# A two-model transformer kernel: its weight ring as one tensor of eight places, and as eight buffers at eight different offsets

## The chip, the cores and the metric

The kernel runs on one core of one Trainium2 chip. The metric is the device time of one launch in microseconds, as the median of three runs. A "slot" below is a piece of the weight stream, not a time.

## What is computed

Two blocks follow each other on a sequence of 256 rows of width 1024, all in float32. The first block has one S5 state-space layer and one attention layer; the second block has two layers with three branches each (latent attention, convolution, retention) and a gated feed-forward part. Cut to what matters here:

```python
def first_block(x, norm_g, ...):
    for i in range(DEPTH):                    # 2
        hn = rms_norm(h, norm_g[i])
        y = s5_mixer(hn, ...) if i % 2 == 0 else moba_mixer(hn, ...)
        h = h + y

def second_block(x, ...):
    for l in range(DEPTH):                    # 2
        h = rms_norm_2(x, ln_mix_pre[l])
        proj = h @ w_in[l]
        ...
        merged = gates[:, :, 0] * y_mla + gates[:, :, 1] * y_conv + gates[:, :, 2] * y_ret
        x = x + rms_norm_2(merged @ w_out[l], ln_mix_post[l])
        h = rms_norm_2(x, ln_ffn_pre[l])
        f = (jax.nn.silu(h @ ffn_w_gate[l]) * (h @ ffn_w_up[l])) @ ffn_w_down[l]
        x = x + rms_norm_2(f, ln_ffn_post[l])
```

Nearly all of the work is the product of 256 rows with some 200 MB of weights, each of which is used once.

## The kernel before

`weight_plan` (the table at the top of the file) cuts all weight matrices into slots in the order in which they are used. A slot is two k-tiles of 128 rows by up to 512 columns: 128 partitions by 1024 numbers, 4 KB in each partition, 512 KB in all. The narrow ones are the slots of the latent projection (two k-tiles by 416 columns) and of the query projection `uq` (384 columns).

Each slot goes through four steps, on four engines, and each engine does its step slot after slot:

- SyncE issues the load of the slot into its place of the ring (L1225, `weights_raw`), once the slot that had the place before is used.
- ScalarE writes the high part, rounded to the TensorE's fast 32-bit type float32r (L1244, `weights_hi<-weights_raw`).
- VectorE writes the rest, the number minus its high part, also in float32r, over the raw numbers (L1776, `weights_lo<-weights_raw,weights_hi`).
- TensorE multiplies. A product is the sum of three: high by high, low by high, high by low.

The activations are kept transposed, also as a high and a low part: `act_F_hi/lo` for most projections, `ffn_F_hi/lo` (hidden part of the feed-forward), `mla_F_hi/lo` and `conv_F_hi/lo`. There are two forms of the product:

- `tile_slot` (L700, L701, L702): the activation tile of 128 by 128 is the stationary operand, the weights are the moving one, 512 columns (416 or 384 in the narrow slots). The profile prints the two in the order moving, stationary: `acc<-weights_hi,act_F_hi`.
- `hidden_slot` (L678, L679, L680): the weights are the stationary operand, 128 by 128, and the activations the moving one, 256 columns. This is the form of the feed-forward's first products, two attention projections and the convolution's input: `acc<-act_F_hi,weights_hi`.

The first 16 slots (`whole_slot`, L639) are multiplied in plain float32 from `weights_raw` against `hn_F`, with no high and low part.

While a matmul streams its moving operand, TensorE already loads the stationary operand of the next one. In `tile_slot` each matmul has another stationary tile than the one before, and so it is in `hidden_slot`.

The ring has six places, `R = 6`, and two more, `R_MORE = 2`, in three stretches of the program in which there is room for them (`weights_hi_more` and so on, the attention, and each layer from its latent heads' end on). `place` gives each slot the place that was filled longest ago. A ring is one tensor `[P, R, SLOT]`; a place is 4096 bytes, so all its places begin at the same offset modulo 512 bytes. `weights_raw` and `weights_lo` lie at the same addresses. Small tensors that nothing reads (`weights_offset` L205, `rows_offset` L261, `latent_rows_offset`, `conv_rows_offset` and `mla_heads`) push what follows them to another offset. The three functions `high`, `whole` and `low` (L233 to L243) give the operand of a slot from its place. Nothing else names the ring.

Of the kernel before, what the change touches and what calls it, by code (L numbers as in the profile page):

```python
# [8 lines left out]
F32 = mybir.dt.float32  # L9
F32R = mybir.dt.float32r  # L10
# [5 lines left out]
P = 128  # L16
# [34 lines left out]
R, R0 = 6, 4  # L51

R_MORE = 2
AHEAD = R - 2
SLOT = 1024

WHOLE = 16

# [11 lines left out]
def weight_plan():  # L70


    chunks = []

    def add(name, n, width, ktiles):
        slots = [(k, min(2, ktiles - k)) for k in range(0, ktiles, 2)]
        for i in range(n):
            chunks.append((f"{name}{i}", width, slots))

    add("ssm_in.", 4, 512, DT)  # L80
    add("glu.", 2, 512, DT)
    add("ssm_out.", 2, 512, DT)
    for i in ATTN_ORDER:
        chunks.append((f"attn_in.{i}", 512, [(k, 2) for k in range(0, DT, 2)]))
    add("attn_out.", 2, 512, DT)
    for l in range(DEPTH2):
        add(f"L{l}.lat.", 1, QR + KVR + ROPE, DT)
        add(f"L{l}.glu.", 2, 512, DT)
        add(f"L{l}.uq.", 2, 384, QR // P)
        add(f"L{l}.ukv.", 2, 512, KVR // P)  # L90
        add(f"L{l}.ret.", 6, 512, DT)
        add(f"L{l}.gate.", 6, 512, DT)
        add(f"L{l}.mla_o.", 2, 512, 4)
        add(f"L{l}.ret_o.", 2, 512, DT)
        add(f"L{l}.conv_o.", 2, 512, 4)
        add(f"L{l}.out.", 2, 512, DT)
        add(f"L{l}.ffn.", HID // FCH, 2 * FCH, DT)
        add(f"L{l}.down.", 2, 512, HT)
    slot, off, table, slots = 0, 0, {}, []
    for c, (name, width, parts) in enumerate(chunks):  # L100
        table[name] = dict(index=c, width=width, first=slot, n=len(parts))
        for k, nk in parts:
            slots.append(dict(chunk=name, k=k, nk=nk, width=width, off=off))
            off += P * nk * width
            slot += 1
    return table, slots, off
# [68 lines left out]
def build(nc, stream, consts, x_in, ssm_ab, ssm_ldt, ssm_bc, rows, qk_gain, positions, decay, conv_p, lat_gain, out):  # L175
    table, slots, _ = weight_plan()
# [16 lines left out]
    with ctx:  # L193
        def sb(name, shape, dt=F32, scope=None):
            return (scope or ctx).enter_context(nc.sbuf_tensor(name, shape, dt))
# [6 lines left out]
        with_channels = [name for name in table if ".ffn." in name or name in ("attn_in.6", "attn_in.7")  # L202
                         or (name[0] == "L" and ".glu." in name)]

        sb("weights_offset", [P, 16])  # L205
        with ExitStack() as s0:
            sb("weights_near", [P, R0, SLOT], F32, s0)
            bcq = sb("ssm_by_pair", [P, 4, Q, GROUP], F32, s0)
        with ExitStack() as s0:
            raw = sb("weights_raw", [P, R, SLOT], F32, s0)  # L210
        w_lo = sb("weights_lo", [P, R, SLOT], F32R)
        with ExitStack() as s0:
            c_alt = sb("c_mats_alt", [P, 4, PQ, SUB * GROUP], F32, s0)
            f0 = sb("hn_F", [P, DT, SEQ], F32, s0)
        w_hi = sb("weights_hi", [P, R, SLOT], F32R)

        begins = [table["attn_in.0"]["start"]] + [table[f"L{l}.lat.0"]["start"] + MLA_END for l in range(DEPTH2)]
        ends = [table[f"L{l}.uq.0"]["start"] for l in range(DEPTH2)] + [NS]
        place, last_in = [], {}
# [8 lines left out]
        for a in begins:  # L228
            for p in range(R, R + R_MORE):
                n = min(n for n in range(a + R, NS) if place[n] == p)  # L230
                before[n] = max(a, before[n] or 0)

        def high(n, cols):  # L233

            return w_hi[:, place[n], cols] if place[n] < R else hi_more[:, place[n] - R, cols]

        def whole(n, cols):

            return raw[:, place[n], cols] if place[n] < R else raw_more[:, place[n] - R, cols]

        def low(n, cols):

            return w_lo[:, place[n], cols] if place[n] < R else lo_more[:, place[n] - R, cols]  # L243
        const = sb("consts", [P, N_CONST])
        ident = const[:, C_ID:C_ID + P]
        xT = sb("x_T", [P, TT, D])
# [11 lines left out]

        sb("rows_offset", [P, 16])  # L261
        with ExitStack() as s0:
            toep = sb("toeplitz", [P, 2, SUB, PCOLS], F32, s0)
        f_hi = sb("act_F_hi", [P, DT, SEQ], F32R)
# [57 lines left out]
        with ExitStack() as s4:  # L322
            latp = sb("lat_gain", [P, QR + KVR], F32, s4)
            cfp = sb("conv_params", [P, 4, TAPS + 3], F32, s4)
            sb("latent_rows_offset", [P, 24], F32, s4)
            mo_hi = sb("mla_F_hi", [P, 4, SEQ], F32R, s4)
            mo_lo = sb("mla_F_lo", [P, 4, SEQ], F32R, s4)
            c_hi, c_lo = mo_hi, mo_lo
            conv_t = sb("conv_tanh", [P, TT, CONV], F32, s4)
            conv_F = sb("conv_in_F", [P, 4, SEQ + 2 * PAD], F32, s4)  # L330
            conv_sum = sb("conv_acc_F", [P, 4, SEQ], F32, s4)
            bns = sb("bn_stats", [P, 10, 8], F32, s4)
            rope_w = conv_t[:, 0, :].rearrange("p (k h d) -> p k h d", k=4, h=MLA_H)
            rqT = sb("ret_q_T", [P, TT, 512], F32, s4)
            rkT = sb("ret_k_T", [P, TT, 512], F32, s4)
            ret_g = sb("ret_g_T", [P, TT, D], F32, s4)
            gates = sb("gates_T", [P, 3, TT, D], F32, s4)

            with ExitStack() as s5:
                cT = sb("lat_T", [P, TT, QR + KVR + ROPE], F32, s5)  # L340
                cnT = sb("lat_norm_T", [P, TT, QR + KVR], F32, s5)
            r_d = sb("r_decay_T", [P, RH, TT, SEQ], F32, s4)
            with ExitStack() as s5:
                mq = sb("mla_q_T", [P, TT, MLA_H, MQK], F32, s5)
                mk = sb("mla_k_T", [P, TT, MLA_H, MQK], F32, s5)
                mv = sb("mla_v_T", [P, TT, MLA_H, MV], F32, s5)
                m_qk = sb("m_qk_F", [P, 2, 512], F32, s5)
                m_p = sb("m_probs", [P, 2, TT, SEQ], F32, s5)
                m_pt = sb("m_probs_T", [P, 2, TT, TT, P], F32, s5)
                m_st = sb("m_stat", [P, 2, 8], F32, s5)  # L350

            with ExitStack() as s6:
                r_qk = sb("r_qk_F", [P, RH, 512], F32, s6)
                r_s = sb("r_scores_T", [P, 2, TT, SEQ], F32, s6)
            with ExitStack() as s6:
                sb("conv_rows_offset", [P, 24], F32, s6)
                cf_hi = sb("conv_F_hi", [P, 4, SEQ], F32R, s6)
                cf_lo = sb("conv_F_lo", [P, 4, SEQ], F32R, s6)
            with ExitStack() as s6:
                sb("mla_heads", [P, 3880], F32, s6)  # L360
                hi_more = sb("weights_hi_more", [P, R_MORE, SLOT], F32R, s6)
                with ExitStack() as s7:
                    raw_more = sb("weights_raw_more", [P, R_MORE, SLOT], F32, s7)
                lo_more = sb("weights_lo_more", [P, R_MORE, SLOT], F32R, s6)
        rv = hT
        gF = hT[:, :, :].rearrange("p t d -> p (t d)").rearrange("p (h q) -> p h q", q=SEQ)

# [866 lines left out]
        def _(act):  # L1234
            pos = 0

            def make_hi(s):
                n = slots[s]["nk"] * slots[s]["width"]
                if s < WHOLE:
                    return  # L1240
                act.wait_ge(raw_in[place[s]], landed(s))
                if s < WHOLE + R:
                    act.wait_ge(slot_used, WHOLE)
                act.activation(high(s, slice(0, n)), whole(s, slice(0, n)), ACT.Copy).then_inc(hi_made, 1)  # L1244
# [1595 lines left out]
```

## Time and profile before

| | us |
|---|---|
| median of 3 runs | 1238.23 |
| lowest, highest | 1234.74, 1239.33 |
| span of the profiled execution | 1235.8 |
| TensorE busy in it | 1205.2 |
| VectorE busy | 901.5 |
| ScalarE busy | 639.1 |
| GpSimd busy | 100.4 |

No time of the profiled execution beyond its span is given; the span lies between the lowest run and the median. Times in the profile are counted from the span's start. The duration that is shown for a matmul (0.39 us for 512 columns) contains its latency, and the next matmul starts before it ends. So what a matmul costs in a stream is the distance from its start to the start of the next, called its pitch here. A row of the timeline is one instruction or several alike in a row; its first number is its start. The distance of two far starts by the number of matmuls between them gives a pitch to a tenth of a nanosecond.

### The profile page before, as it was taken

To read this page: it belongs to the slowest core of one execution; us is meant where nothing else is said; L and a number is where in the kernel's file an instruction comes from. 1 tells how busy PE (TensorE), PEld (TensorE's weight loads), DVE (VectorE), ACT (ScalarE), POOL (GpSimd) and SP (SyncE) were. 2 spreads that over 40 slices of the span, in tenths; PEclk is the share of its full clock that TensorE was granted. 3 is DMA by queue.
4 is the path that set the end of the run, shared out by engine and by line. 5 is a ranking of instruction groups with operands and counts; after the bars stand their busy time and mean duration, and the time that the engine had idled before them with its cause. 6 is when DMAs were issued, how large, how long until landed. Compare 5 with 4: busy or idle time off the path is not lost.

```text
span 1235.8 us, 19035 instructions
## 1 busy us (share of the span) xinstructions
PE 1205.2 (98%) x7597; PEld 1013.5 (82%) x7597; DVE 901.5 (73%) x1463; ACT 639.1 (52%) x1034; POOL 100.4 (8%) x163
## 2 busy tenths in 40 slices
PE   7999999999999999999999999999999999999998
PEld 3566778888988788787999987988788787999986
DVE  7998877757589998687666655589997687665553
ACT  4334565665556665545444544556575545444441
POOL 6300011101000200201000001000200201000000
PEclk9999999999999999999999999999999999999999
DMA  7635666434565555354766664565445355565552
GB/s 251 221 94 173 205 208 191 156 119 146 163 205 168 155 157 187 133 169 164 216 201 188 193 195 154 174 211 169 158 153 188 132 170 170 190 197 193 191 194 75
DMA packets 71958, 215.68 MB, mean 175 GB/s; under 512 B 16256, under 2 KB 19744, under 8 KB 71744
## 3 DMA queue, kind: packets, MB, share of 16 engines
q1 hardware_dynamic: 65008, 206.37, 52.0%
q0 software_dynamic: 2112, 6.97, 1.8%
q10 hardware_dynamic: 4752, 1.14, 0.4%
q8 instruction: 60, 0.98, 0.3%
q14 instruction: 26, 0.21, 0.1%
HBM read 208.95 MB, written 3.15 MB: 172 GB/s over the span
## 4 chain that ended last, share of the span: by engine, by line
PE 86%; DVE 8%; ACT 3%; issue 2%; POOL 1%; DMA 0%; DVEq 0%; POOLq 0%; ACTq 0%
PE acc L700 17%; PE acc L702 17%; PE acc L701 17%; PE acc L678 7%; PE acc L680 7%; PE acc L679 7%; PE acc L639 3%; PE mixed L1015 1%; DVE weights_lo L1776 1%; PE mixed L1112 1%; ACT junk L1279 1%; PE turned L755 1%; DVE h_T L1806 1%; PE mixed L999 1%; PE mixed L1008 1%
## 5 line engine op out<-in xcount | busy, mean ns | idle before, releaser
L1776 DVE TENSOR_TENSOR weights_lo<-weights_raw,weights_hi 128x1024 fp32r<-128x1024 f32 (+1 forms) x304 | 355.7, 1204 | 71.6 <-ACT weights_hi L1244 71.0
L1244 ACT ACTIVATE weights_hi<-weights_raw 128x1024 fp32r<-128x1024 f32 (+1 forms) x304 | 305.8, 1043 | 80.8 <-DMA weights_raw<-stream_dram 80.6
L700 PE MATMUL acc<-weights_hi,act_F_hi 128*128 128x512 f32 (+1 forms) x680 | 275.7, 406 | 5.6 <-DVE act_F_lo L1806 3.4
L702 PE MATMUL acc<-weights_hi,act_F_lo 128*128 128x512 f32 (+1 forms) x680 | 267.2, 393 | 0.0
L701 PE MATMUL acc<-weights_lo,act_F_hi 128*128 128x512 f32 (+1 forms) x680 | 265.4, 390 | 0.0
L678 PE MATMUL acc<-act_F_hi,weights_hi 128*128 128x256 f32 x624 | 173.6, 278 | 0.0
L679 PE MATMUL acc<-act_F_hi,weights_lo 128*128 128x256 f32 x624 | 172.5, 276 | 0.0
L680 PE MATMUL acc<-act_F_lo,weights_hi 128*128 128x256 f32 x624 | 172.4, 276 | 0.0
L700 PEld LDWEIGHTS acc<-weights_hi,act_F_hi 128*128 128x128 f32 x680 | 128.7, 189 | 34.2 <-DVE act_F_lo L1806 4.3
L702 PEld LDWEIGHTS acc<-weights_hi,act_F_lo 128*128 128x128 f32 x680 | 128.4, 189 | 28.4
L701 PEld LDWEIGHTS acc<-weights_lo,act_F_hi 128*128 128x128 f32 x680 | 128.7, 189 | 25.6
L679 PEld LDWEIGHTS acc<-act_F_hi,weights_lo 128*128 128x128 f32 x624 | 117.2, 188 | 0.2
L678 PEld LDWEIGHTS acc<-act_F_hi,weights_hi 128*128 128x128 f32 x624 | 117.1, 188 | 0.2
L680 PEld LDWEIGHTS acc<-act_F_lo,weights_hi 128*128 128x128 f32 x624 | 117.2, 188 | 0.0
L1806 DVE SCALAR_TENSOR_TENSOR conv_acc_F<-conv_in_F,conv_params,conv_acc_F 128x256 f32<-128x256 f32 x240 | 97.9, 477 | 0.0
L1776 DVE TENSOR_TENSOR weights_lo_more<-weights_raw_more,weights_hi_more 128x1024 fp32r<-128x1024 f32 (+1 forms) x60 | 71.4, 1214 | 18.2 <-ACT weights_hi_more L1244 18.1
L1806 DVE SCALAR_TENSOR_TENSOR ffn_tanh_F<-ffn_tanh_F,acc 128x512 f32<-128x512 f32 (+1 forms) x24 | 15.4, 643 | 89.4 <-ACT ffn_tanh_F L1364 84.8
L1244 ACT ACTIVATE weights_hi_more<-weights_raw_more 128x1024 fp32r<-128x1024 f32 (+1 forms) x60 | 61.9, 1048 | 26.8 <-DMA weights_raw_more<-stream_dram 26.8
L1364 ACT ACTIVATE ffn_tanh_F<-acc 128x512 f32<-128x512 f32 x20 | 12.0, 598 | 111.3 <-PE acc L680 111.3
L639 PE MATMUL acc<-weights_raw,hn_F 128*128 128x512 f32 x128 | 59.9, 615 | 1.0 <-ACT hn_F L1380 1.0
L678 PE MATMUL acc<-act_F_hi,weights_hi_more 128*128 128x256 f32 x208 | 57.7, 277 | 0.0
L680 PE MATMUL acc<-act_F_lo,weights_hi_more 128*128 128x256 f32 x208 | 57.4, 276 | 0.0
(339 smaller groups left out, 1923.6 us busy)
## 6 DMA issues: line engine op xcount, KB each, us to landing
weights_raw<-stream_dram SPq DMA_DIRECT2D x306, 512.0 KB, 3.7
weights_raw_more<-stream_dram SPq DMA_DIRECT2D x58, 512.0 KB, 4.3
gains<-rows_dram POOLq DMA_DIRECT2D x12, 512.0 KB, 4.8
weights_raw<-stream_dram SPq DMA_DIRECT2D x6, 416.0 KB, 3.1
weights_raw<-stream_dram SPq DMA_DIRECT2D x4, 384.0 KB, 3.5
x_T<-x_in_dram SPq DMA_DIRECT2D x4, 256.0 KB, 6.0
ssm_bc<-ssm_bc_dram SPq DMA_DIRECT2D x1, 1024.0 KB, 8.6
u_scratch<-u_T ACTq DMA_DIRECT2D x4, 256.0 KB, 5.5
```

What stands on the lines that cost most here:

```text
L639: i = pe.matmul(acc[par][t][:, 0:w], f0[:, k, t * P:(t + 1) * P], whole(pos, slice(kk * w, (kk + 1) * w)), start=first and kk == 0, stop=l ...
L678: pe.matmul(o, wh, hi[:, k, :], start=first and kk == 0 and m % 2 == 0, stop=False, skip_group_check=True)
L679: pe.matmul(o, wl, hi[:, k, :], start=False, stop=False, skip_group_check=True)
L680: i = pe.matmul(o, wh, lo[:, k, :], start=False, stop=last and kk == s["nk"] - 1, skip_group_check=True)
L700: pe.matmul(o, xh, wh, start=first and kk == 0, stop=False)
L701: pe.matmul(o, xh, wl, start=False, stop=False)
L702: i = pe.matmul(o, xl, wh, start=False, stop=last and kk == s["nk"] - 1)
L755: i = pe.transpose(turned_bank[n % 2][:, kk * P:(kk + 1) * P], src(t, 4 * half + kk), ident)
L999: x = pe.transpose(b[0:dk, (2 * n + t) * P:(2 * n + t + 1) * P], src(t, i), ident)
L1244: act.activation(high(s, slice(0, n)), whole(s, slice(0, n)), ACT.Copy).then_inc(hi_made, 1)
L1776: dve.tensor_tensor(low(s, slice(0, n)), whole(s, slice(0, n)), high(s, slice(0, n)).bitcast(F32), ALU.subtract).then_inc(lo_made, 1)
L1806: return dve.scalar_tensor_tensor(out=o, in0=a, scalar=s, in1=b, op0=op0, op1=op1)
```

## The change

The tensors of the ring become lists of tensors, one for each place: a to f for the six, g and h for the two more. Each but the last of a list is 16 numbers (64 bytes) longer than a slot, so that the next place begins 64 bytes further modulo 512. The padding tensor before the ring goes; one of 8 numbers now stands between the low and the high part; `rows_offset` goes; the two places g and h get paddings so that they continue the rows of offsets. No instruction is added, removed or moved: on all five engines the same instructions stand in the same order with the same waits, and the loads have the same sizes. Only addresses differ.

```diff
+LINE = 16
...
-        sb("weights_offset", [P, 16])
+        def places(names, kind, dt, scope=None):
+
+            return [sb(f"weights_{kind}_{c}", [P, SLOT + LINE], dt, scope) for c in names[:-1]] + [
+                sb(f"weights_{kind}_{names[-1]}", [P, SLOT], dt, scope)]
+
         with ExitStack() as s0:
-            sb("weights_near", [P, R0, SLOT], F32, s0)
+            sb("weights_near", [P, R0, SLOT + LINE], F32, s0)
             bcq = sb("ssm_by_pair", [P, 4, Q, GROUP], F32, s0)
         with ExitStack() as s0:
-            raw = sb("weights_raw", [P, R, SLOT], F32, s0)
-        w_lo = sb("weights_lo", [P, R, SLOT], F32R)
+            raw = places("abcdef", "raw", F32, s0)
+        w_lo = places("abcdef", "lo", F32R)
+        sb("weights_offset", [P, 8])
...
-        w_hi = sb("weights_hi", [P, R, SLOT], F32R)
+        w_hi = places("abcdef", "hi", F32R)
...
-            return w_hi[:, place[n], cols] if place[n] < R else hi_more[:, place[n] - R, cols]
+            return w_hi[place[n]][:, cols] if place[n] < R else hi_more[place[n] - R][:, cols]
...
-        sb("rows_offset", [P, 16])
...
-                sb("mla_heads", [P, 3880], F32, s6)
-                hi_more = sb("weights_hi_more", [P, R_MORE, SLOT], F32R, s6)
+                sb("mla_heads", [P, 3912], F32, s6)
+                hi_more = places("gh", "hi", F32R, s6)
+                sb("low_offset", [P, 24], F32, s6)
                 with ExitStack() as s7:
-                    raw_more = sb("weights_raw_more", [P, R_MORE, SLOT], F32, s7)
-                lo_more = sb("weights_lo_more", [P, R_MORE, SLOT], F32R, s6)
+                    raw_more = places("gh", "raw", F32, s7)
+                lo_more = places("gh", "lo", F32R, s6)
```

`whole` and `low` change as `high` does. Where the tensors begin, in bytes modulo 512:

| | before | after |
|---|---|---|
| raw and low part, places a to h | 192 in all | 128, 192, 256, 320, 384, 448, 0, 64 |
| high part, places a to h | 192 in all | 480, 32, 96, 160, 224, 288, 352, 416 |
| `act_F_hi/lo`, `ffn_F_hi/lo`, `conv_F_hi/lo` | 128 | 160 |
| `mla_F_hi/lo` | 256 | 288 |
| `hn_F` | 192 | 480 |

A k-tile of 512 columns, a tile of 128 columns and a k-tile of activations are whole multiples of 512 bytes, so within a slot these offsets hold for every operand. The second k-tile of a slot of 416 columns begins 1664 bytes in, which is 128 modulo 512.

## Rows read from the trace of the kernel before

**Rows 1.** The page: the span, TensorE's share, and its granted clock in 40 slices.

```profile
span 1235.8 us, 19035 instructions
...
PE 1205.2 (98%) x7597; PEld 1013.5 (82%) x7597; DVE 901.5 (73%) x1463; ACT 639.1 (52%) x1034; POOL 100.4 (8%) x163
...
PEclk9999999999999999999999999999999999999999
```

**Rows 2.** The page: the chain that ended last, by engine.

```profile
PE 86%; DVE 8%; ACT 3%; issue 2%; POOL 1%; DMA 0%; DVEq 0%; POOLq 0%; ACTq 0%
```

**Rows 3.** TensorE's groups by line and shape: count | busy us, mean ns | idle before.

```profile
L700 PE MATMUL acc<-weights_hi,act_F_hi 128*128 128x512 f32 x656 | 267.0, 407 | 5.4 <-DVE act_F_lo L1806 3.4 <-DVE weights_lo L1776 2.0
...
L678 PE MATMUL acc<-act_F_hi,weights_hi 128*128 128x256 f32 x624 | 173.6, 278 | 0.0
...
L678 PE MATMUL acc<-act_F_hi,weights_hi_more 128*128 128x256 f32 x208 | 57.7, 277 | 0.0
...
L700 PE MATMUL acc<-weights_hi,ffn_F_hi 128*128 128x512 f32 x144 | 55.9, 388 | 0.0
...
L700 PE MATMUL acc<-weights_hi,mla_F_hi 128*128 128x512 f32 x24 | 9.6, 402 | 0.0
```

**Rows 4.** TensorE's waits: for which instruction, us in total, times, longest.

```profile
PE acc L700 <- DVE weights_lo L1776: 2.2, 5, 0.7
```

**Rows 5.** Timeline, feed-forward's second product of layer 0: first and last matmul.

```profile
702.99 0.39 PE L700 MATMUL acc<-weights_hi,ffn_F_hi 128*128 128x512 f32 x1
...
763.18 0.40 PE L702 MATMUL acc<-weights_hi,ffn_F_lo 128*128 128x512 f32 x1
```

**Rows 6.** Timeline, product with `mla_F` in layer 0: second and last matmul of a stretch.

```profile
507.34 0.39 PE L701 MATMUL acc<-weights_lo,mla_F_hi 128*128 128x512 f32 x1
...
512.47 0.39 PE L702 MATMUL acc<-weights_hi,mla_F_lo 128*128 128x512 f32 x1
```

**Rows 7.** Timeline, a slot of 416 columns: second k-tile from 307.50, first of the next from 308.06.

```profile
307.50 0.35 PE L700 MATMUL acc<-weights_hi,act_F_hi 128*128 128x416 f32 x1
...
308.06 0.35 PE L700 MATMUL acc<-weights_hi,act_F_hi 128*128 128x416 f32 x1
...
308.63 0.35 PE L700 MATMUL acc<-weights_hi,act_F_hi 128*128 128x416 f32 x1
```

**Rows 8.** Timeline, `hidden_slot` in layer 0's feed-forward: first and last matmul of a stretch.

```profile
605.17 0.28 PE L679 MATMUL acc<-act_F_hi,weights_lo 128*128 128x256 f32 x1
...
702.87 0.28 PE L680 MATMUL acc<-act_F_lo,weights_hi_more 128*128 128x256 f32 x1
```

**Rows 9.** Busy us (and instructions) of each engine in stretches, then clock, DMA share, GB/s.

```profile
core 0: us, PE busy (x) PEld busy (x) DVE busy (x) ACT busy (x) POOL busy (x), PEclk, DMA share, GB/s
702.99:763.18 60.19, 60.19 (x265) 49.40 (x264) 31.60 (x31) 26.83 (x35) 1.57 (x4) 1.00 0.57 173
605.17:702.87 97.70, 97.70 (x864) 97.70 (x863) 58.66 (x63) 44.15 (x54) 0.00 (x0) 1.00 0.64 194
507.34:512.47 5.13, 5.13 (x23) 4.11 (x22) 2.77 (x6) 3.64 (x9) 2.95 (x6) 1.00 0.24 68
...
754.97:758.11 3.14, 3.14 (x15) 2.60 (x14) 0.00 (x0) 0.00 (x0) 0.00 (x0) 1.00 0.03 10
736.99:740.48 3.49, 3.49 (x17) 2.87 (x16) 3.49 (x4) 2.27 (x3) 0.00 (x0) 1.00 0.73 181
```

**Rows 10.** Timeline, a stretch with the other engines idle, and one with them busy.

```profile
737.09 0.39 PE L702 MATMUL acc<-weights_hi,ffn_F_lo 128*128 128x512 f32 x1
...
740.29 0.39 PE L701 MATMUL acc<-weights_lo,ffn_F_hi 128*128 128x512 f32 x1
...
755.17 0.39 PE L700 MATMUL acc<-weights_hi,ffn_F_hi 128*128 128x512 f32 x1
...
757.92 0.39 PE L700 MATMUL acc<-weights_hi,ffn_F_hi 128*128 128x512 f32 x1
```

**Rows 11.** The page: the two steps that make the parts of a slot, and its load.

```profile
L1776 DVE TENSOR_TENSOR weights_lo<-weights_raw,weights_hi 128x1024 fp32r<-128x1024 f32 (+1 forms) x304 | 355.7, 1204 | 71.6 <-ACT weights_hi L1244 71.0
L1244 ACT ACTIVATE weights_hi<-weights_raw 128x1024 fp32r<-128x1024 f32 (+1 forms) x304 | 305.8, 1043 | 80.8 <-DMA weights_raw<-stream_dram 80.6
...
weights_raw<-stream_dram SPq DMA_DIRECT2D x306, 512.0 KB, 3.7
```

More of the change, by code:

```diff
@@ L233, in high @@
         def high(n, cols):
-            return w_hi[:, place[n], cols] if place[n] < R else hi_more[:, place[n] - R, cols]
+            return w_hi[place[n]][:, cols] if place[n] < R else hi_more[place[n] - R][:, cols]
         def whole(n, cols):
-            return raw[:, place[n], cols] if place[n] < R else raw_more[:, place[n] - R, cols]
+            return raw[place[n]][:, cols] if place[n] < R else raw_more[place[n] - R][:, cols]
         def low(n, cols):
-            return w_lo[:, place[n], cols] if place[n] < R else lo_more[:, place[n] - R, cols]
+            return w_lo[place[n]][:, cols] if place[n] < R else lo_more[place[n] - R][:, cols]
         const = sb("consts", [P, N_CONST])
```

## The prediction

> **What bounds the kernel.** I read the page first: TensorE is busy for 1205.2 of 1235.8 us, at the full clock in all slices [rows 1], and the chain that ended last runs through it for 86% of the span [rows 2]. Its waits come next: for the low part of a slot, the last product of the ring's pipeline, it waits 2.2 us in all [rows 4]. So neither loads, nor ScalarE, nor VectorE set the pace: the time is the number of matmuls by their pitch. The change leaves the instructions as they are, so it can only act through the pitch, or by making the pipeline of the ring so slow that TensorE waits.
>
> For the pitch I went to the timeline. In the feed-forward's second product, 264 matmuls of 512 columns start between 702.99 and 763.18 us: 60.19 us by 263 steps is **228.9 ns** [rows 5]. At the upper of TensorE's two clocks (2.4 GHz, granted in full there [rows 9]) 512 columns are 213.3 ns; 15.6 ns are left over. In the hidden form 97.70 us by 862 steps (864 instructions of the window less two still running at its start) is **113.3 ns** for 256 columns [rows 8, 9], with 6.7 ns left over. What these leftovers hang on is the whole question.
>
> **Do the other engines make them?** The places of the ring now all begin at the same offset, so one could think that TensorE, reading one place, meets ScalarE, VectorE or a load in the same part of another. The trace has a clean test of it. From 754.97 to 758.11 us VectorE, ScalarE and GpSimd are idle and the DMA share is 0.03; 12 steps there take 2.75 us, 229.2 ns each. From 736.99 to 740.48 us VectorE is busy all the time, ScalarE for 2.27 us, the DMA share is 0.73; 14 steps take 3.20 us, 228.6 ns each [rows 9, 10]. The other engines cost a matmul nothing that I can see.
>
> **Do TensorE's own two reads make them?** While a matmul streams its moving operand, the next stationary one is loaded. I call relation the start of the moving operand minus that of the stationary one being loaded, modulo 512 bytes. Before, it is 64 for the tile form (192 minus 128), except 448 with `mla_F` (192 minus 256), 192 in the second k-tile of a 416-column slot, and 448 in the hidden form (128 minus 192). With `mla_F`, 5.13 us by 22 steps is 233.2 ns [rows 6, 9]: 4.3 ns more than at relation 64. In the slots of 416 columns three steps at relation 192 take 0.56 us and the next three, at relation 64, 0.57 us [rows 7]; that is 186.7 against 190.0 ns, 3.3 less at 192, known only to some 3 ns since starts are given to 10 ns. So the relation does matter, by some 2% of a matmul between the best and the worst of three, and this is what the change spreads.
>
> The Trainium skill says otherwise: its page "SBUF — State Buffer", section "Who interferes with whom", gives TensorE two independent read ports, one for the moving operand and one for the weight load, and says that it never waits on anyone. By that the sum would be exactly zero. The two pitches at the same shape speak against it, the quiet stretch for its other half.
>
> **The terms.** After the change the relation of the high part takes, over the places a to h, 320, 384, 448, 0, 64, 128, 192 and 256: all eight. The low part takes eight that lie half-way between them (480, 32, 96, 160, 224, 288, 352, 416). Only 64, 192 and 448 have rows. I take the mean of these three as the mean of all.
>
> - Tile form at 64: 656, 80, 144, 32 and 32 instructions of L700 with 512 columns (the largest and one other in [rows 3]), 944, by the three lines, 2832 matmuls. The three relations give 228.9, 225.6 (3.3 less, from the 416-column rows) and 233.2: mean 229.2. 2832 by 0.3 ns is **+0.9 us**. Bounds: all at the best, 2832 by -3.3, -9.3 us; all at the worst, 2832 by 4.3, +12.2 us. I take the mean since the places are used in turn.
> - Tile form with `mla_F`: 24 and 16 by three, 120 matmuls, from 233.2 to 229.2: **-0.5 us**. Slots of 416 columns: 96 matmuls that had one good and one middling relation and get the mean: 0, within 96 by 4 ns, 0.4 us. Those of 384 columns: 48, likewise within 0.2 us.
> - Hidden form: 624 and 208 instructions of L678 [rows 3], by three 2496 matmuls at 113.3 ns, at relation 448. That is the worst of the three in the tile form, whose leftover is 19.9 ns there and 15.9 in the mean, a factor of 0.8. If the leftover of 6.7 ns shrinks alike, a matmul gains 1.3 ns: **-3.3 us**. Here the roles are exchanged and no row shows another relation. Lower bound: the leftover shrinks as 12.3 to 19.9 at the best relation, 2.6 ns, -6.5 us. Upper bound: nothing excludes that 448 is good in this form, so the same 2.6 ns upwards, +6.5 us. I take the middle of the gain, since the direction of the difference is the same.
> - The first 16 slots in plain float32, transposes and attention: their operands' relations change too, but 128 matmuls and small shapes are all; 0, within 1 us.
> - ScalarE and VectorE: both work inside one place; the high part now begins 352 bytes further modulo 512 than the raw one. L1776 takes 1204 ns and L1244 1043 [rows 11]. Even 3% on both, some 35 ns, on a slot that lasts 12 matmuls (2.7 us) is covered: VectorE is idle for 71.6 us ahead of this very step, and TensorE waits 2.2 us for it. If that cover went, 364 slots by 35 ns would be 13 us; I cost it at 0. The loads have the same size, still begin at multiples of 64 bytes, and 3.7 us to landing are covered by the ring's depth.
>
> Sum: 0.9 - 0.5 - 3.3 = **-2.9 us**, on a span of 1235.8: 1232.9. The median is 2.4 us above this execution's span, so 1235.3 on the scale of the runs.
>
> **Rival 1, slower: the relations without rows are the bad ones.** Two streams that begin in step (relation 0, and 32 and 480 next to it) may collide longest, and 448 is the nearest to them with a row, and the worst. If five of eight relations cost what 448 does, the tile form pays five eighths of 12.2 us, +7.6; if in the hidden form 448 was a good one and it pays 1.3 ns, +3.2 us. Together +10.8: 1249. For it: the trend from 192 to 64 to 448. Against it: the worst seen is only 4.3 ns. It decides once the mean pitch in the stretch of [rows 5] is above 231 ns.
>
> **Rival 2, faster: most relations are as good as 192.** Then the tile form gains 2.5 ns, -7.1 us, and the hidden one the full 2.6 ns, -6.5 us: 1224.6. For it: 192 lies in the wide gap of five values without rows, and is best; against it: one shape of 96 matmuls carries it.
>
> **Rival 3, faster: the leftovers are collisions with the other engines after all**, and spreading the places removes them: 15.6 ns by 2832 and 6.7 by 2496, up to -61 us, 1177. The quiet stretch speaks against it. The page "TensorE: Matmul & The Clock Gate", section "Back-to-back issue gap" of the Trainium skill, gives 2.5 ns over the columns' time as the gap of a lone stream; its sum here would be some 37 us for the tile form, as an estimate, if something could remove the rest. The trace never shows it for this type.
>
> **Rival 4, nothing at all:** the pitch is a matter of the operands' other properties, `mla_F` differing by chance of its place: 1238.2.
>
> **The numbers.** About what a measurement of this kernel can tell from no change is 0.5%, 6.2 us. My forecast, near the middle, 0.34, and rival 4, 0.06, fall within it, though their own spread leaks to both sides; rival 1 has 0.30, rival 2 0.27, rival 3 0.03. With the leaks this makes 0.32 for faster, 0.36 for the same and 0.32 for slower. The cases of both signs hold most of the chance; the forecast's own range is 1230 to 1241. The whole range reaches from beyond rival 2, 1221, to beyond rival 1, 1255: below lies the tile form's lower bound with the hidden one's (-15.8, 1222), above both upper bounds (+18.7, 1257), not quite reached.
>
> **What would show it.** The clock, the number of instructions and the waits should stay as they are. In the timeline of the feed-forward's second product the pitch should no longer be the same from slot to slot but go through a cycle with the places: groups of 12 matmuls near 226, 229 and 233. If all of them stay at 228.9, rival 4 holds. The hidden stretch of 862 steps should fall from 97.70 to about 96.6 us; if it is above 98, the exchange of roles was the mistake. Stretches with `mla_F` should come down on the mean. If TensorE's wait for the low part grows beyond some 5 us, the cost of L1776 and L1244 was mis-sized. A pitch that changes within a slot with what ScalarE or VectorE does would overturn the argument from the quiet stretch.

## The result and the profile after

The changed kernel takes 1251.78 us (median of 4 runs, 1251.5 to 1253.75), the kernel before 1238.78 on the same chip (4 runs, 1234.74 to 1241.58). The ratio is 1.0118, with a 95% interval of 1.01 to 1.0137: **slower by 1.2%**. The forecast was 1235.3, a gain of 2.9 us; what came is a loss of 13.0 us. The time lies inside the stated range, near its upper end, and within 3 us of rival 1.

The page after, the lines that answer to [rows 1] and [rows 2]:

```profile
span 1251.9 us, 19035 instructions
...
PE 1223.8 (98%) x7597; PEld 1025.6 (82%) x7597; DVE 902.2 (72%) x1463; ACT 637.6 (51%) x1034; POOL 100.4 (8%) x163
...
PEclk9999999999999999999999999999999999999999
...
PE 87%; DVE 8%; ACT 3%; issue 1%; POOL 1%; DMA 0%; DVEq 0%; POOLq 0%; ACTq 0%
```

The instructions are as many, the granted clock is 0.994 over the span where it was 0.995, VectorE and ScalarE are as busy as before to 1.5 us. Only TensorE is busy longer, by 18.6 us, on a span that is 16.1 us longer; the difference is idle time of TensorE that is gone. (The spans differ by more than the medians, since the trace before is of one of the faster executions and the trace after is of the slowest of its four, 1253.75 us.) The line numbers of the changed kernel are 8 higher there: L686 to L688 are the hidden form, L708 to L710 the tile form.

The timeline after, the first and last matmul of the two stretches of [rows 8] and [rows 5]:

```profile
609.13 0.28 PE L687 MATMUL acc<-act_F_hi,weights_lo_a 128*128 128x256 f32 x1
...
710.32 0.28 PE L688 MATMUL acc<-act_F_lo,weights_hi_h 128*128 128x256 f32 x1
710.43 0.40 PE L708 MATMUL acc<-weights_hi_c,ffn_F_hi 128*128 128x512 f32 x1
...
771.55 0.40 PE L710 MATMUL acc<-weights_hi_b,ffn_F_lo 128*128 128x512 f32 x1
```

The hidden form's 862 steps take 101.19 us, 117.4 ns each, where they took 97.70, 113.3 ns. The tile form's 263 steps take 61.12 us, 232.4 ns each, against 228.9. By 2496 matmuls the first is 10.2 us; by 2832 the second is 9.9 us at most, if the other stretches of the tile form lost as much. Together they cover the 18.6 us.

The description of the tile form ahead is wrong in one thing. Its matmuls of L708 and L709 (L700 and L701 before) use the same stationary tile, the high part of the activations, and only L710 has another one. The page shows as many weight loads as matmuls all the same, 7597 each [rows 1]. So what holds in both forms is that each matmul has a load of its own, and not that each has another tile.

Busy time of each engine in three stretches after: one in which only TensorE works, the hidden stretch and the tile stretch.

```profile
core 0: us, PE busy (x) PEld busy (x) DVE busy (x) ACT busy (x) POOL busy (x), PEclk, DMA share, GB/s
762.90:766.36 3.46, 3.46 (x16) 2.81 (x15) 0.00 (x0) 0.00 (x0) 0.00 (x0) 1.00 0.06 24
609.13:710.32 101.19, 101.19 (x865) 101.19 (x863) 58.66 (x63) 44.13 (x54) 0.00 (x0) 1.00 0.60 187
710.43:771.55 61.12, 61.12 (x266) 49.47 (x264) 31.60 (x31) 26.82 (x35) 1.67 (x4) 1.00 0.56 169
```

The timeline of the first of them, with the other engines idle:

```profile
763.17 0.39 PE L710 MATMUL acc<-weights_hi_f,ffn_F_lo 128*128 128x512 f32 x1
...
766.18 0.40 PE L708 MATMUL acc<-weights_hi_e,ffn_F_hi 128*128 128x512 f32 x1
```

Thirteen steps take 3.01 us, 231.5 ns each. The same quiet stretch before had 229.2 [rows 10]. So the loss is there also with VectorE, ScalarE and GpSimd idle and a DMA share of 0.06. All of these steps but the first are in places a and b, whose slots take 231.1 and 232.2 ns a matmul over both layers, so the quiet has made them no faster. And TensorE's waits for the low part have not grown: 2.0 us in five waits, against 2.2 in five before [rows 4]. What VectorE and ScalarE need for a slot is the same within 1%, here for place a:

```profile
PE acc L708 <- DVE weights_lo_c L1784: 0.8, 2, 0.6
...
PE acc L708 <- DVE weights_lo_d L1784: 0.6, 1, 0.6
...
PE acc L708 <- DVE weights_lo_b L1784: 0.6, 2, 0.3
...
L1784 DVE TENSOR_TENSOR weights_lo_a<-weights_raw_a,weights_hi_a 128x1024 fp32r<-128x1024 f32 (+2 forms) x51 | 61.5, 1205 | 11.7 <-ACT weights_hi_a L1252 11.7
...
L1252 ACT ACTIVATE weights_hi_a<-weights_raw_a 128x1024 fp32r<-128x1024 f32 (+2 forms) x51 | 53.2, 1043 | 12.7 <-DMA weights_raw_a<-stream_dram 12.7
```

### The profile page after: what moved, and what is told of

Read it like the earlier page. It is cut to its first block, busy times and chain, and to the rows that moved or that the text cites. A ratio compares the mean times of both kernels' runs of the same rounds, so it can differ in the third digit from the quotient of the medians.

```text
span 1251.9 us, 19035 instructions
## 1 busy us (share of the span) xinstructions
PE 1223.8 (98%) x7597; PEld 1025.6 (82%) x7597; DVE 902.2 (72%) x1463; ACT 637.6 (51%) x1034; POOL 100.4 (8%) x163
## 4 chain that ended last, share of the span: by engine, by line
PE 87%; DVE 8%; ACT 3%; issue 1%; POOL 1%; DMA 0%; DVEq 0%; POOLq 0%; ACTq 0%
PE acc L708 17%; PE acc L709 17%; PE acc L710 17%; PE acc L688 8%; PE acc L687 8%; PE acc L686 7%; PE acc L647 3%; PE mixed L1023 1%; PE mixed L1120 1%; ACT junk L1287 1%; PE turned L763 1%; PE mixed L1007 1%; PE mixed L1016 1%; DVE h_T L1814 1%; DVE junk L1817 1%
## 5 line engine op out<-in xcount | busy, mean ns | idle before, releaser
L1784 DVE TENSOR_TENSOR weights_lo_c<-weights_raw_c,weights_hi_c 128x1024 fp32r<-128x1024 f32 (+2 forms) x51 | 61.8, 1211 | 19.9 <-ACT weights_hi_c L1252 19.4
L1784 DVE TENSOR_TENSOR weights_lo_e<-weights_raw_e,weights_hi_e 128x1024 fp32r<-128x1024 f32 (+3 forms) x50 | 59.9, 1198 | 16.6 <-ACT weights_hi_e L1252 16.6
L1784 DVE TENSOR_TENSOR weights_lo_a<-weights_raw_a,weights_hi_a 128x1024 fp32r<-128x1024 f32 (+2 forms) x51 | 61.5, 1205 | 11.7 <-ACT weights_hi_a L1252 11.7
L1784 DVE TENSOR_TENSOR weights_lo_b<-weights_raw_b,weights_hi_b 128x1024 fp32r<-128x1024 f32 (+2 forms) x51 | 61.4, 1205 | 9.5 <-ACT weights_hi_b L1252 9.5
L1784 DVE TENSOR_TENSOR weights_lo_d<-weights_raw_d,weights_hi_d 128x1024 fp32r<-128x1024 f32 (+2 forms) x51 | 61.7, 1209 | 8.7 <-ACT weights_hi_d L1252 8.5
L1784 DVE TENSOR_TENSOR weights_lo_f<-weights_raw_f,weights_hi_f 128x1024 fp32r<-128x1024 f32 (+3 forms) x50 | 59.9, 1198 | 5.5 <-ACT weights_hi_f L1252 5.4
L1252 ACT ACTIVATE weights_hi_b<-weights_raw_b 128x1024 fp32r<-128x1024 f32 (+2 forms) x51 | 53.2, 1043 | 18.2 <-DMA weights_raw_b<-stream_dram 17.9
L1252 ACT ACTIVATE weights_hi_d<-weights_raw_d 128x1024 fp32r<-128x1024 f32 (+2 forms) x51 | 53.4, 1046 | 15.5 <-DMA weights_raw_d<-stream_dram 15.4
L1252 ACT ACTIVATE weights_hi_a<-weights_raw_a 128x1024 fp32r<-128x1024 f32 (+2 forms) x51 | 53.2, 1043 | 12.7 <-DMA weights_raw_a<-stream_dram 12.7
L1252 ACT ACTIVATE weights_hi_c<-weights_raw_c 128x1024 fp32r<-128x1024 f32 (+2 forms) x51 | 53.4, 1047 | 11.5 <-DMA weights_raw_c<-stream_dram 11.5
L708 PE MATMUL acc<-weights_hi_c,act_F_hi 128*128 128x512 f32 (+1 forms) x116 | 48.2, 416 | 1.5 <-DVE weights_lo_c L1784 0.8
L708 PE MATMUL acc<-weights_hi_a,act_F_hi 128*128 128x512 f32 (+1 forms) x116 | 47.9, 413 | 0.8 <-DVE act_F_lo L1814 0.8
L708 PE MATMUL acc<-weights_hi_d,act_F_hi 128*128 128x512 f32 (+1 forms) x116 | 46.6, 402 | 0.6 <-DVE weights_lo_d L1784 0.6
L708 PE MATMUL acc<-weights_hi_b,act_F_hi 128*128 128x512 f32 (+1 forms) x116 | 46.3, 399 | 0.6 <-DVE weights_lo_b L1784 0.6
L708 PE MATMUL acc<-weights_hi_e,act_F_hi 128*128 128x512 f32 (+1 forms) x108 | 44.5, 412 | 1.7 <-DVE act_F_lo L1814 1.7
L710 PE MATMUL acc<-weights_hi_c,act_F_lo 128*128 128x512 f32 (+1 forms) x116 | 46.1, 397 | 0.0
```

The lines of the kernel that those rows point to most:

```text
L708: pe.matmul(o, xh, wh, start=first and kk == 0, stop=False)
L710: i = pe.matmul(o, xl, wh, start=False, stop=last and kk == s["nk"] - 1)
L1784: dve.tensor_tensor(low(s, slice(0, n)), whole(s, slice(0, n)), high(s, slice(0, n)).bitcast(F32), ALU.subtract).then_inc(lo_made, 1)
```

## The experiments

The change does several things at once, and four theories could explain what it did:

- **A, half lines:** the activations and the high part now begin 32 bytes into a 64-byte line, and an operand that does so is slower.
- **B, parts apart:** the high and the low part of a slot no longer lie at the same offset, and the switch between them costs.
- **C, spread:** it costs that successive slots lie at different offsets.
- **D, relation:** each relation of moving to stationary operand has its own pitch; before, the common one was a good one, and the eight average worse.

All twelve kernels differ from the one before or from the change in paddings alone; they compute the same with the same instructions in the same order. In each the pitch was read in the two stretches of layer 0, as above. All results in one table; "tile" and "hidden" are ns for a matmul, the relations are in bytes modulo 512, for the high and then the low part where they differ. The experiments were made in three rounds, on three chips, and each ratio is to the kernel before in the same round. The pitches of the table are those of two stretches of one execution each; that one kernel can have more than one pitch at the same offsets comes below.

| run | tile relation | tile ns | hidden ns | median us | ratio to before (95%) |
|---|---|---|---|---|---|
| before | 64 | 228.9 | 113.3 | 1237 to 1239 | |
| the change | eight, parts apart | 232.4 | 117.4 | 1251.78 | 1.0118 (1.01 to 1.0137) |
| uniform_shift32 | 64 | 228.9 | 113.3 | 1237.58 | 1.0 (0.9987 to 1.0014) |
| uniform_parts352 | 64, 224 | 229.0 | 117.0 | 1247.55 | 1.0071 (1.0056 to 1.0086) |
| uniform_parts320 | 64, 256 | 233.3 | 117.8 | 1256.49 | 1.0156 (1.0122 to 1.019) |
| spread_lines64 | eight, parts apart | 230.7 | 117.6 | 1248.51 | 1.0079 (1.0064 to 1.0094) |
| spread_parts_alike | six values | 231.8 | 118.2 | 1253.27 | 1.0111 (1.0088 to 1.0135) |
| uniform_relation0 | 0 | 226.8 | 120.0 | 1246.37 | 1.0056 (1.0037 to 1.0074) |
| uniform_relation192 | 192 | 233.3 | 117.8 | 1255.22 | 1.0123 (1.0096 to 1.0151) |
| uniform_relation320 | 320 | 228.9 | 113.3 | 1237.42 | 0.9988 (0.997 to 1.0005) |
| uniform_relation128 | 128 | 232.4 | 118.7 | 1256.22 | 1.0141 (1.0112 to 1.0169) |
| uniform_relation32 | 32 | 233.3 | 118.3 | 1256.62 | 1.0145 (1.0121 to 1.0169) |
| spread_by_256 | 64 and 320 | 228.9 | 113.3 | 1238.11 | 1.0002 (0.9986 to 1.0018) |
| narrow_buffers_at_0 | 64; 0 for three | 226.7 | 113.4 | 1236.21 | 0.9986 (0.9973 to 0.9999) |

### First four: what is it in the change?

The whole layout 32 bytes further, against the kernel before:

```diff
-        sb("weights_offset", [P, 16])
+        sb("weights_offset", [P, 24])
```

> The ring as before (one offset for all places, high and low part alike), but the ring, the activations and all behind them lie 32 bytes further: weights at 224, activations at 160 modulo 512, relation 64 as before. Theory A (an operand that begins half-way in a 64-byte line costs a matmul more, since after the change the high parts and the activations begin 32 bytes into such a line): the hidden stretch slows to about 117.5 ns a matmul and the tile form to about 232, the time is 1250 or more. Theory B (what costs is that the high and the low part of a slot no longer have the same relation to the activations) and theory C (what costs is that the places differ): no change, 113.3 and 229 ns, 1238.

The time and both pitches are those of before. Theory A is out in this form: at relation 64, it does not matter whether the operands begin at whole lines or half-way into them.

The parts apart, in a ring of one offset for all places. The second kernel has 80 and 48 for 88 and 40:

```diff
         w_lo = sb("weights_lo", [P, R, SLOT], F32R)
+        sb("high_offset", [P, 88])
...
+                sb("low_offset", [P, 40], F32, s6)
```

> The ring as before, all places alike, but the high part begins 352 bytes further than the low one modulo 512, as after the change: low 192, high 32, activations 480; so the relation is 64 for the high part and 224 for the low one in every slot, what place e has after the change. High part and activations lie 32 bytes into a 64-byte line, the low part does not. Theory B (parts apart) and theory A (half lines): as slow as the change, about 117 ns hidden, 232 ns tile form, 1250. Theory C (only the spread over the places costs): 113.3 and 229 ns, 1238.

> As the run with the parts 352 bytes apart, but 320 apart, so that every operand begins at a multiple of 64 bytes: low 192, high 0, activations 448; relation 64 for the high part, 256 for the low. Theory A (half lines): as fast as before, 113.3 and 229 ns, 1238. Theory B (parts in different relations): slow, about 117 and 232 ns, 1250. Theory C: as fast as before.

Both are slow, 1.0071 and 1.0156, without any spread: theory C is not needed. At 320 bytes, all operands at whole 64-byte lines, it is even worse than at 352. That fits B, but D as well, since the low part now has another relation to the activations (256 or 224) than before.

The 229.0 ns of the run with 352 bytes do not speak for its whole tile form. A stretch of it with `act_F`, at the same two relations, goes otherwise:

```profile
172.46 0.39 PE L703 MATMUL acc<-weights_lo,act_F_hi 128*128 128x512 f32 x1
...
215.39 0.40 PE L704 MATMUL acc<-weights_hi,act_F_lo 128*128 128x512 f32 x1
```

These are 184 steps in 42.93 us, 233.3 ns each, in the same execution.

The change with all operands at whole lines:

```diff
-        sb("weights_offset", [P, 8])
+        sb("weights_offset", [P, 16])
...
-                sb("low_offset", [P, 24], F32, s6)
+                sb("low_offset", [P, 16], F32, s6)
```

> The change with 32 more bytes between the low and the high parts: eight places at eight offsets as in the change, but every operand now at a multiple of 64 bytes (low part from 128 on, high part from 0 on, activations at 192). Theory A (half lines): back to 1238, 113.3 and 229 ns. Theory B (parts apart) and theory C (spread): stays near 1251, about 117 and 232 ns.

Slow too, 1.0079, though a third less so than the change: the tile form has 230.7 ns against 232.4. So relations of half a line seem to matter a little more than those of whole lines; the first run had excluded only that an operand's own place matters. (The two kernels were timed in different rounds, each against the kernel before.)

### Next four: parts apart or relation?

The parts alike again, the places spread. The gap is 64 bytes behind places a, b and c, and 320 bytes between the low and the high part:

```diff
+        LO_GAPS, HI_GAPS = [16, 16, 16, 0, 0, 0], [16, 16, 16, 0, 0, 0]
...
-        sb("weights_offset", [P, 8])
+        sb("weights_offset", [P, 80])
...
-                sb("low_offset", [P, 24], F32, s6)
+                sb("low_offset", [P, 112], F32, s6)
```

> Places at different offsets, but the high and the low part of a place at the same one: places a, b, c at 128, 192, 256, places d, e, f at 320, g at 384, h at 448; activations at 192. Relations of the tile form 448, 0, 64, 128, 128, 128, 192, 256; of the hidden form 64, 0, 448, 384, 384, 384, 320, 256. Theory B (parts apart are what costs): every place has about 340 ns for its three hidden matmuls and 687 for its three of the tile form, the time is about 1238. Theory D (the relation itself costs, in the hidden form above all; 448 is a good one): places with hidden relation 448 (c) have 340 ns, others such as 0 and 384 about 353 to 357; the time is about 1248.

1.0111, as slow as the change, with the parts alike. So the parts need not be apart for the loss. The spread alone could still make it here (theory C), as the parts alone could in the two runs before; the next three runs have neither. The places have pitches of their own. The timeline of this run, at the first matmul of six slots of 24 matmuls each (g, h; and later g, h, c, d):

```profile
614.05 0.28 PE L688 MATMUL acc<-act_F_hi,weights_hi_g 128*128 128x256 f32 x1
...
616.87 0.28 PE L688 MATMUL acc<-act_F_hi,weights_hi_h 128*128 128x256 f32 x1
...
636.81 0.28 PE L688 MATMUL acc<-act_F_hi,weights_hi_g 128*128 128x256 f32 x1
...
639.53 0.28 PE L688 MATMUL acc<-act_F_hi,weights_hi_h 128*128 128x256 f32 x1
...
642.41 0.28 PE L688 MATMUL acc<-act_F_hi,weights_hi_c 128*128 128x256 f32 x1
...
645.24 0.28 PE L688 MATMUL acc<-act_F_hi,weights_hi_d 128*128 128x256 f32 x1
```

Place h (hidden relation 256) takes 2.88 us for its 24, 120.0 ns each. Place c has the relation of the kernel before, 448, and yet takes 2.83 us, 117.9 ns. And place g (320) takes 2.82 us the first time, 117.5 ns, and 2.72 us the second, 113.3 ns. So a relation does not quite fix the pitch: some have two.

The ring in one piece, and the activations moved, with all that lies behind them, by `rows_offset`; `mla_heads` changes with it, so that places g and h keep their offset. Here 32 stands for relation 0; 112 gives 192, 80 gives 320:

```diff
-        sb("rows_offset", [P, 16])
+        sb("rows_offset", [P, 32])
...
-                sb("mla_heads", [P, 3880], F32, s6)
+                sb("mla_heads", [P, 3864], F32, s6)
```

> The ring as before, parts alike, only the activations moved 64 bytes on: weights and activations both at 192, relation 0 in both forms. Theory B: 1238, as before. Theory D: hidden form at about 354 ns for three, 1250 or so.

> The ring as before, parts alike, activations at 0: relation 192 in the tile form (the one that was the fastest in the 416-column slots before), 320 in the hidden form. Theory B: about as before, or a little faster by the tile form (3 ns by 2832 matmuls, 1229). Theory D: hidden form (320, which is 64 modulo 256) at about 355 ns for three, plus 12 us, minus what the tile form gains: 1240 to 1252.

> The ring as before, parts alike, activations at 384: relation 320 in the tile form, 192 in the hidden form. If relations repeat after 256 bytes (theory D with the good hidden places of the spread with 64-byte lines: high part at 192 or 448), the hidden form stays at 340 ns, the tile form at 687 and the time at 1238. If they repeat after 512 only, 192 is the opposite of the good one and the hidden form costs 350 or more. Theory B: 1238.

Theory D holds in all three: with the parts alike and all places alike, both pitches change at relations 0 and 192, and at 320 they are back. Relation 0 is the best for the tile form, 226.8 ns, and the worst for the hidden one, 120.0; its timeline, first and last of the two stretches:

```profile
603.26 0.28 PE L679 MATMUL acc<-act_F_hi,weights_lo 128*128 128x256 f32 x1
...
706.70 0.28 PE L680 MATMUL acc<-act_F_lo,weights_hi_more 128*128 128x256 f32 x1
706.82 0.40 PE L700 MATMUL acc<-weights_hi,ffn_F_hi 128*128 128x512 f32 x1
...
766.46 0.39 PE L702 MATMUL acc<-weights_hi,ffn_F_lo 128*128 128x512 f32 x1
```

103.44 us for the hidden stretch is 5.74 more than before, and 59.64 us for the tile stretch 0.55 less. Relation 192 was expected to help the tile form, by the slots of 416 columns; it has 233.3 ns there, more than 0, 64 and (below) 128. Relation 320 has the pitches of 64 in layer 0, so for these relations the pattern repeats after 256 bytes. Two more values agree: in spread_parts_alike, place h, at hidden relation 256, has the 120.0 ns of relation 0, and `mla_F` before, at tile relation 448, has the 233.2 of 192.

The 320 run also shows the second pitch at work. In its profiled execution, which took 1242.06 us, the two stretches of layer 0 are fast and the same stretches of layer 1 slow:

```profile
604.97 0.28 PE L679 MATMUL acc<-act_F_hi,weights_lo 128*128 128x256 f32 x1
...
702.66 0.28 PE L680 MATMUL acc<-act_F_lo,weights_hi_more 128*128 128x256 f32 x1
...
1071.15 0.28 PE L679 MATMUL acc<-act_F_hi,weights_lo 128*128 128x256 f32 x1
...
1172.67 0.28 PE L680 MATMUL acc<-act_F_lo,weights_hi_more 128*128 128x256 f32 x1
1172.80 0.40 PE L700 MATMUL acc<-weights_hi,ffn_F_hi 128*128 128x512 f32 x1
...
1234.16 0.39 PE L702 MATMUL acc<-weights_hi,ffn_F_lo 128*128 128x512 f32 x1
```

97.69 us against 101.52, with every operand at the same offset and with the same instructions: a stretch falls into one of two steady rhythms where it begins (113.3 or 117.8 ns) and keeps it for its 862 steps. The tile form has two as well: behind the slow hidden stretch, its 263 steps take 61.36 us, 233.3 ns each, where layer 0 has 228.9. Together the two stretches make 5.0 us of the 6.8 by which the ten runs of this kernel differ (1235.26 to 1242.06).

This bears on the table. 117.8 and 233.3 ns, the slow rhythm at relation 320, are also the values of relation 192 and of uniform_parts320, and 233.3 is that of relation 32. So a value of the table is the rhythm in which a kernel was found, and no run shows whether one of these three has a faster one too. What speaks for the relation is that the time goes with it: the lowest runs of these three kernels are 1252.0, 1254.8 and 1255.6 us, and none of the 80 runs of the kernels whose common relations are 64 and 320 (the kernel before, uniform_shift32, uniform_relation320, spread_by_256) is above 1243.8.

### Last four: the period, the rest of the classes, and a version to keep

Spread again, parts apart again, but all by 256 bytes:

```diff
+        LO_GAPS, HI_GAPS = [0, 0, 64, 0, 0, 0], [0, 0, 64, 0, 0, 0]
+
+        sb("ring_offset", [P, 16])
...
-        sb("weights_offset", [P, 8])
...
+        sb("rows_offset", [P, 16])
...
-                sb("low_offset", [P, 24], F32, s6)
+                sb("low_offset", [P, 64], F32, s6)
```

> Places and parts spread again, but only by 256 bytes: low part of places a, b, c at 192 and of d, e, f at 448, the high part the other way round, g at 192 and h at 448, activations at 128. So the high and the low part of each place lie 256 bytes apart modulo 512, and the places differ, but modulo 256 every relation is that of the kernel before. Theory D with a period of 256 bytes: 340 and 687 ns for three matmuls in nearly all slots, 1238. Theory B or C, or a period of 512: 350 and 695, 1248 or more.

1.0002, with 113.3 and 228.9 ns. The timeline of its hidden stretch and of the tile stretch behind it:

```profile
603.15 0.28 PE L690 MATMUL acc<-act_F_hi,weights_lo_a 128*128 128x256 f32 x1
...
700.85 0.28 PE L691 MATMUL acc<-act_F_lo,weights_hi_h 128*128 128x256 f32 x1
700.96 0.39 PE L711 MATMUL acc<-weights_hi_c,ffn_F_hi 128*128 128x512 f32 x1
...
761.16 0.40 PE L713 MATMUL acc<-weights_hi_b,ffn_F_lo 128*128 128x512 f32 x1
```

This is the cleanest of the twelve: eight separate buffers at two offsets, each with its parts 256 bytes apart, and the time is that of before. Where spreading and parting leave all relations the same modulo 256, they cost nothing. (The slow rhythm turns up here too: the 96 hidden matmuls from 591.28 to 602.47 us, just ahead of this stretch, take 117.8 ns each.)

Without `rows_offset` the activations lie at 64, relation 128; with 24 numbers at 160, relation 32 (`mla_heads` follows as above):

```diff
-        sb("rows_offset", [P, 16])
```

> The last of the four classes modulo 256, parts alike, places alike: activations at 64, relation 128 in the tile form and 384 in the hidden one. Theory D, from the places of the spread with parts alike: 698 ns for three of the tile form, 356 in the hidden form; 1238 + 944 x 11 ns + 832 x 16 ns = about 1262.

> Parts and places alike, activations at 160: relation 32 in the tile form, 480 in the hidden one, half-way between the classes 0 and 64. Theory D, if what counts changes smoothly: tile form between 680 and 687 ns for three, hidden form between 340 and 360, 1242. If it is the change's half lines that hold the worst values: hidden form above 360, tile form above 700.

Relation 128 is slow in both forms, as expected, if less than forecast (1256.22 instead of about 1262). Relation 32 is not half-way between its neighbours: 233.3 ns in the tile form, where 0 and 64 have 226.8 and 228.9. So the curve is not smooth, and the one relation of half a line that was measured is bad for the tile form. (For the low part alone this is not so plain: with it at 224, uniform_parts352 had 229.0 ns in one product and 233.3 in another.) After the change all low parts stood in relations of half a line.

Last, the activations that are only ever stationary, moved to the best relation of the tile form:

```diff
         with ExitStack() as s3:
+            sb("ffn_offset", [P, 16], F32, s3)
...
-            sb("latent_rows_offset", [P, 24], F32, s4)
+            sb("latent_rows_offset", [P, 8], F32, s4)
...
-                sb("conv_rows_offset", [P, 24], F32, s6)
+                sb("conv_rows_offset", [P, 56], F32, s6)
...
-                sb("mla_heads", [P, 3880], F32, s6)
+                sb("mla_heads", [P, 3896], F32, s6)
```

> The kernel before with the activations that are only ever stationary (hidden part of the feed-forward, latent heads, convolution output) moved to the offset of the weights, 192, so relation 0 for them; the ring, and the activations that the hidden form also reads, as before. Theory D: 176 x 3 matmuls with ffn_F go from 687 to about 681 ns for three, 32 with conv_F likewise, 40 with mla_F from 700 to about 681: -1.1, -0.2 and -0.8 us, 2 us in all (0.17%). Theory B: nothing.

1236.21 us (12 runs) against 1237.34 (23 runs), 0.9986 with an interval of 0.9973 to 0.9999: 0.14% less, near the expected 2 us, but at the edge of what the interval can tell. The pitch shows the effect more clearly: 226.7 instead of 228.9 ns over the tile stretch. The time by itself does not settle it: the lowest run of the kernel before, 1235.35 us, is below the lowest here, 1235.56, and part of the difference of the medians may be the mix of rhythms in the executions.

## Why the prediction was wrong

**Right: what bounds the kernel, and where the change acts.** TensorE's busy time carried the whole difference, ScalarE, VectorE and the loads none of it; the terms of ScalarE, VectorE and the loads, costed at 0, were 0. That the other engines cost a matmul nothing (the quiet stretch) was confirmed by the quiet stretch after, where the loss is there without them. Rival 3, 0.03, was rightly small. Rival 4 is refuted: with the ring as before and the activations moved against it, both pitches moved. The Trainium skill's page "SBUF — State Buffer", section "Who interferes with whom", gives TensorE an independent port for each of its two reads and says that it never waits on anyone. Here the pitch does depend on how the two operands lie to each other, 226.8 to 233.3 ns for one shape, and the runs decide. By what mechanism, and whether at the ports, no run shows.

**Wrong: "I take the mean of these three as the mean of all."** The three relations 64, 192 and 448 are only two classes modulo 256, since 192 and 448 are the same. The tile form has 228.9 ns in the first and 233.3 in the second. That 192 looked good came from the slots of 416 columns; for 512 columns it has the highest value of the four classes. So the 225.6 ns that I gave to relation 192 were 7.7 ns off, and the same shape's own value at 448, 233.2, would have been right. The mean over the four classes, measured one by one, is (226.8 + 228.9 + 232.4 + 233.3) / 4 = 230.4, which the run with whole lines comes near (230.7); the low part in half-line relations (233.3 in the one measured) makes it (2 x 230.4 + 233.3) / 3 = 231.4, and 232.4 was measured. The term was +0.9 us, and it came out at up to +9.9. The term of `mla_F`, -0.5 us, came out at 0: the 22 steps from 509.81 to 514.94 us after take 233.2 ns each, as before.

**Wrong: the hidden form, "the leftover shrinks alike".** I carried the order of the relations over from the tile form. The hidden form has its own: 113.3 ns at 448, 117.8 at 320, 118.7 at 384, 120.0 at 0, mean 117.5; measured after the change, 117.4. The kernel before sat at the best of them, in its trace also in the faster rhythm, and could only lose. The term was -3.3 us, and it was +10.2, beyond even the upper bound of +6.5.

**Rival 1** was the nearest in time (1249 against 1251.78) and the right one by its point of decision: the stretch of [rows 5] has a mean pitch of 232.4, above 231. That it came so near in time was partly luck, since its two terms were 7.6 and 3.2 us where the pitches make up to 9.9 and 10.2. In mechanism it was half right. Bad relations were the majority, but it had relation 0 as the bad one for the tile form, where it is the best; and 1.3 ns for the hidden form was a third of what came. The cycle of slots near 226, 229 and 233 ns that I had named as the sign to look for is there only in small: by place, the slots of this product take from 231.1 ns (a) to 233.2 (d and h) a matmul, and none is near 226 or 229.

What stays open: why a relation costs what it does. No run separates the relation to the stationary operand being loaded from that to the one in use, since in the tile form both begin alike. The pure mean also does not explain everything. With the low part at 256 and the high one at 64, classes with 226.8 and 228.9 ns by themselves, the tile form had 233.3 (uniform_parts320), the value of the slow rhythm. So either the sequence of relations counts too, and theory B has some truth as a second effect, or it helps to decide the rhythm; no run separates the two. And which of its rhythms a stretch takes, in either form, was seen, not controlled.

## What to carry to other kernels

Where a stream of matmuls loads its stationary operand anew each time, its pitch can depend on where the two operands lie to each other: compute start to start over a few hundred of them, and move one buffer by 64 bytes at a time over 256 bytes before trusting a layout. Read more than one stretch, and take several executions, since the same layout can run in two rhythms. Spreading buffers over offsets took about the average of all relations here, or somewhat worse; one good relation for all, chosen for each form of product by itself, is better. And a value read from one shape (416 columns here), or for one form, does not carry over to another.

## What the runs showed of the hardware that I had not expected

- The pitch goes with the relation modulo 256 bytes and not with the place itself, where it was tried: 113.3 and 228.9 ns at tile relation 64 and at 320, and with everything moved by 32 bytes.
- The same relation is worth different things in the two forms: the tile form at relation 0 is the best (226.8 ns), the hidden form at 0 the worst (120.0), 5.9% above its best.
- The same stretch has two steady pitches at the same offsets, 113.3 and 117.8 ns in the hidden form and 228.9 and 233.3 in the tile form (uniform_relation320, layers 0 and 1). It keeps one for up to a hundred microseconds, and the time of one layer's two stretches moves by 5.0 us with it.
